# Layer 0 of a two-layer hybrid decoder trunk: VectorE's work, the weight loads and ScalarE's sums in another order up to the scan

## What is computed

```python
h = rmsnorm(x, norm_mix[i])
z = h @ w_in[i]
y_ssm = ssm_branch(z[..., :c0], ...) @ w_ssm_out[i]          # complex diagonal state space model
y_att = dilated_attention(z[..., c0:c1], ..., positions, ...) @ w_att_out[i]   # masks, rotary angles
mem_n = rmsnorm(mem, norm_mem[i])
y_mem = memory_attention(z[..., c3:c4], mem_n, w_mem_kv[i], ...) @ w_mem_out[i]
...
x = x + merged @ w_o[i]
h2 = rmsnorm(x, norm_ffn[i])
x = x + swiglu(...)          # layer 0: dense; layer 1: top 2 of 8 experts
```

## Time and profile before

| | us |
|---|---|
| median of 3 runs | 1813.82 (1813.15 to 1814.66) |
| profiled execution, its own time | 1815.75 |
| its span, first to last instruction | 1813.8 |
| PE busy in the span | 1762.2 (97%) |
| DVE busy | 1442.5 (80%) |
| ACT busy | 1175.7 (65%) |
| mean granted TensorE clock | 0.993 |

### The profile page before, as it was taken

How to read it: one execution, slowest core, us unless ns; L and a number is a source line. 1 busy time by engine, 2 the same in 40 slices (tenths; PEclk the granted TensorE clock), 3 DMA queues, 4 the chain that set the end, 5 groups by cost and what they waited for, 6 DMA issues and landing times.

```text
span 1813.8 us, 23378 instructions
## 1 busy us (share of the span) xinstructions
PE 1762.2 (97%) x8755; PEld 1457.4 (80%) x8755; DVE 1442.5 (80%) x1336; ACT 1175.7 (65%) x1322; POOL 113.9 (6%) x159
## 2 busy tenths in 40 slices
PE   7799999999999999999999999999999999999998
PEld 5687878888887878887888878888878888888886
DVE  7987557677756954668899888898888998988987
ACT  6467564654455665556776767777767767777775
POOL 3341000122001300000000000000000000000000
PEclk9899999999999999999999999999999999999999
DMA  6344434755544443377999999999999999999994
GB/s 207 116 140 139 139 117 161 229 188 185 184 139 142 149 134 132 118 253 290 371 366 335 371 335 365 366 347 354 377 320 372 365 336 372 357 369 373 350 373 186
DMA packets 227630, 477.17 MB, mean 263 GB/s; under 512 B 16012, under 2 KB 40712, under 8 KB 227528
## 3 DMA queue, kind: packets, MB, share of 16 engines
q1 hardware_dynamic: 227144, 474.99, 73.8%
q0 software_dynamic: 288, 0.79, 0.2%
q10 hardware_dynamic: 96, 0.02, 0.0%
HBM read 474.71 MB, written 1.05 MB: 262 GB/s over the span
## 4 chain that ended last, share of the span: by engine, by line
PE 90%; DVE 4%; ACT 2%; issue 1%; SPq 1%; DMA 1%; DVEq 0%; ACTq 0%
PE ps L694 27%; PE ps L696 27%; PE ps L695 27%; PE ps L1175 1%; PE ps L942 1%; DVE lo L2221 1%; PE ps L914 1%; PE ps L1153 1%; PE ps L873 1%; PE ps L687 1%; DVE ring_lo L1823 1%; PE ps L925 1%; DMA ring<-in_w_mem_kv 1%; ACT hi_m L1309 1%; SPq L420 1%
## 5 line engine op out<-in xcount | busy, mean ns | idle before, releaser
L2221 DVE TENSOR_TENSOR lo<-ring_e,hi 128x2048 fp32r<-128x2048 f32 x288 | 657.8, 2290 | 89.9 <-ACT hi L1590 87.7
L1590 ACT ACTIVATE hi<-ring_e 128x2048 fp32r<-128x2048 f32 x288 | 552.0, 1917 | 172.2 <-PE ps L696 171.7
L694 PE MATMUL ps<-hi,xe_hi 128*128 128x512 f32 x896 | 356.4, 398 | 6.9 <-issue 6.9
L696 PE MATMUL ps<-hi,xe_lo 128*128 128x512 f32 x896 | 350.9, 392 | 0.0
L695 PE MATMUL ps<-lo,xe_hi 128*128 128x512 f32 x896 | 350.4, 391 | 0.0
L1309 ACT ACTIVATE hi_m<-ring 128x1024 fp32r<-128x1024 f32 x160 | 160.7, 1054 | 166.0 <-PE ps L696 157.7
L1823 DVE TENSOR_TENSOR ring_lo<-ring,hi_m 128x1024 fp32r<-128x1024 f32 x160 | 190.6, 1233 | 35.0 <-ACT hi_m L1309 34.5
L694 PEld LDWEIGHTS ps<-hi,xe_hi 128*128 128x128 f32 x896 | 169.1, 189 | 43.5 <-issue 8.3
L696 PE MATMUL ps<-hi_m,xT_lo 128*128 128x512 f32 (+1 forms) x528 | 204.0, 386 | 0.0
L696 PEld LDWEIGHTS ps<-hi,xe_lo 128*128 128x128 f32 x896 | 168.9, 189 | 36.6
L695 PEld LDWEIGHTS ps<-lo,xe_hi 128*128 128x128 f32 x896 | 169.2, 189 | 33.5
(11 more groups left out here) (398 smaller groups left out, 2494.4 us busy)
## 6 DMA issues: line engine op xcount, KB each, us to landing
ring_e<-in_moe_w_gate SPq DMA_DIRECT2D x104, 1024.0 KB, 6.7
ring_e<-in_moe_w_up SPq DMA_DIRECT2D x96, 1024.0 KB, 6.8
ring_e<-in_moe_w_down SPq DMA_DIRECT2D x88, 1024.0 KB, 6.2
ring<-in_w_in SPq DMA_DIRECT2D x50, 1024.0 KB, 5.1
hT<-in_moe_w_down SPq DMA_DIRECT2D x24, 1024.0 KB, 6.7
hT<-in_moe_w_up SPq DMA_DIRECT2D x16, 1024.0 KB, 6.0
ring<-in_ffn_w_gate SPq DMA_DIRECT2D x22, 512.0 KB, 4.0
ring<-in_ffn_w_up SPq DMA_DIRECT2D x22, 512.0 KB, 5.0
```

Of the source, the lines that this page charges most:

```text
L694: nc.tensor.matmul(o, x_hi, w_hi, start=first, stop=False, skip_group_check=True)
L696: return nc.tensor.matmul(o, x_lo, w_hi, start=False, stop=end, skip_group_check=True)
L1590: nc.scalar.activation(hi[:, m % H, :], src, ACT.Copy).then_inc(sem("hi_ready"), 1)
L2221: last = V.tensor_tensor(lo[:, m % H, :], src, hi[:, m % H, :].bitcast(F32), ALU.subtract)
```

## The change

It changes the order of work in layer 0 before the scan; no instruction is added or left out. On SP the positions are loaded fourth, before the second half of the small gains, and tile 3 directly after tile 2, ahead of `load_matrices` and of the broadcasts. On VectorE `constants()` and `rotary_angles()` come before `setup()`, and the rest of tile 7 between `table_coarse` and `table_fine`. On ScalarE the sums of squares of the memory tokens stand after the rotary sines, those of `x` after the high part of tile 4; the high part of tile 3 comes ahead of `input_transposed` and `take_memory(0)`. On GpSimd the masks' second bound comes ahead of `ssm_zeros`, and the first part of `second_matrices` ahead of the reciprocal root for `x`.

```diff
@@ block.sync
                 sp.dma_start(par_rows[i * L * KD:(i + 1) * L * KD, :], ...)
+            sp.dma_start(pos_i[:], positions.rearrange("o (c p) -> p (o c)", p=P)).then_inc(sem("pos_loaded"), 16)
...
             sp.dma_start(x[:], x_in[0].rearrange("(c p) d -> p c d", p=P)).then_inc(sem("x_loaded"), 16)
-            load(2, mix_tiles(0)[2])
-            sp.dma_start(pos_i[:], positions.rearrange("o (c p) -> p (o c)", p=P)).then_inc(sem("pos_loaded"), 16)
+            for i in range(2, R + 1):
+                load(i, mix_tiles(0)[i])
             load_matrices(nc.sync, 0)
...
-                    if l > 0 or i >= R:
+                    if l > 0 or i > R:
                         load(BASE[l] + i, src)
@@ block.gpsimd
-            def second_matrices(l):
+            def second_input(l):
...
                 nc.gpsimd.memset(mT[:], 0.0).then_inc(sem("mT_zero"), 1)
+
+            def second_output(l):
+
...
+            pool.wait_ge(sem("grid_ready"), 1)
+            for c in range(C):
+                for g in range(NG):
+                    last = nc.gpsimd.affine_select(out=gmask(c, g), ...)
+            last.then_inc(sem("mask_ready"), 1)
             ssm_zeros(0)
...
             for l in range(L):
+                if l == 0:
+                    second_input(0)
                 rsqrt_mean(rs[:, 2:2 + C], ss[:, 2:2 + C], D, (sem("x_squared"), 2 * l + 1), sem("x_rs"))
                 if l == 0:
-                    pool.wait_ge(sem("grid_ready"), 1)
...
-                    second_matrices(0)
+                    second_output(0)
@@ block.scalar
                     nc.scalar.activation(dt16[:], dt16[:], ACT.Exp).then_inc(sem("dt_ready"), 1)
-                    act.wait_ge(sem("mem_loaded"), 16)
-                    sum_squares(0, h, "mem_squared", z)
-                    act.wait_ge(sem("x_loaded"), 16)
-                    act.wait_ge(sem("mem_squared"), 1)
-                    sum_squares(2, x, "x_squared", z)
                     weights_high(l)
...
                     nc.scalar.activation(rope[:, 0], turns[:], ACT.Sin, scale=-1.0,
                                          bias=half_pi[:]).then_inc(sem("rope_ready"), 1)
+                    sum_squares(0, h, "mem_squared", z)
+                    weights_high(l)
+                    act.wait_ge(sem("mem_squared"), 1)
                     input_transposed()
                     take_memory(0)
-                    weights_high(l)
                     act.wait_ge(sem("transposed_used"), batches_to(l, "h"))
                     from_batch(coefficients_moves)
                     weights_high(l)
+                    sum_squares(2, x, "x_squared", z)
                 weights_high(l)
@@ block.vector
                 state_rates(l)
-                rotary_angles()
                 weights_low(l)
...
                 table_coarse(l)
+                weights_low(l)
                 table_fine()
                 table_folds()

             def ssm(l):
-                weights_low(l)
+                if l > 0:
+                    weights_low(l)
...
+            constants()
+            rotary_angles()
             setup()
-            constants()
             for l in range(L):
                 ssm_setup(l)
```

More of the change, by code:

```diff
@@ L629, in _ @@
                                               base=SPAN - c * P, pattern=[[1, (c + 1) * P]], channel_multiplier=-1))
+            pool.wait_ge(sem("grid_ready"), 1)
+            for c in range(C):
+                for g in range(NG):
+                    last = nc.gpsimd.affine_select(out=gmask(c, g), in_=gmask(c, g), compare_op=ALU.is_ge, fill=NEG,
+                                                   base=c * P, pattern=[[-1, (c + 1) * P]], channel_multiplier=1)
+            last.then_inc(sem("mask_ready"), 1)
             ssm_zeros(0)
@@ L668, in _ @@
                     ssm_zeros(1)
-                    second_matrices(1)
+                    second_input(1)
+                    second_output(1)
                     rotary_gains(1)
@@ L1413, in mixer @@
                     state_steps(l)
-                if l == 0:
                     act.wait_ge(sem("rope_angle_ready"), 1)
```

## The result

The changed kernel is **slower**: 1822.02 us median of 7 runs (1819.62 to 1823.34) against 1814.91 us of the kernel before in the same session (7 runs, 1813.15 to 1816.71). The ratio is 1.0033, with a 95% interval of [1.0023, 1.0042], just above the 0.2% that can be told from no change; in us the interval is 4.2 to 7.6. The forecast was 1813.6 us with a range to 1816.4; both the sign and the size are wrong. The profiled run took 1819.62 us; its span is 1817.7 us, against 1813.8 before.

What follows compares the result with a forecast made beforehand. VectorE's chain before the scan was taken to bound the kernel: its end at 76.3 - 1.1 - 1.0 + 2.3 = 76.5 us, tile 8 ending at 90.4 instead of 90.57, gain 0.2, hence 1813.6 us, range 1809.4 to 1816.4.

Steps and rivals of the forecast that it cites:

- the large wait: TensorE's 9.64 us idle until the rest of tile 7; forecast to move to tile 8 as 10 to 12 us.
- the tail behind F: ScalarE's work after VectorE's last fold; tile 8 can't start before 6.3 us later, then takes 7.6 us.
- F: End of VectorE's nearly gapless work before the scan, at its last fold: 76.3 us before, 76.5 forecast.
- the landing of tile 4: SP's load of tile 4 lands at 37.6 us; ScalarE waits 4.4 us, leaving 1.1 of 5.6 us gained.
- the upper bound of 1.5: Delay of `setup()` on VectorE behind constants and angles: 0.6 us forecast, at most 1.5 if positions land at 7.3.
- The sequence that I copied from the kernel before: SP's six matrix loads, four broadcasts and one tile: 14.5 us from tile 3's landing to tile 4's.
- The second rival: SP held 8.5 us by the second `b` matrix's load; tile 4 lands at 42.3, 1818.3 us; chance 0.1.
- The take-back from GpSimd: Less contention on VectorE as GpSimd's second `b` matrices end before tile 5: 1.0 us gained, bounds 0 and 1.8.
- ScalarE's cover: 1.6 us by which tile 3's first half on ScalarE (25.7) precedes VectorE's need for it (27.3).
- The sums are free: ScalarE's sums of squares of the memory tokens, 4.4 us, moved after the sines, cost no time.

Runs made afterwards that it cites:

- two experiments: Against the changed kernel: tile 3 issued where it was before, 1817.70 us (1.0010 to before); the four broadcasts behind tile 5, 1816.17 us (1.0007).
- The second session: The changed kernel unaltered, timed once more against the kernel before: 1819.45 us median against 1815.52, ratio 1.0027 [1.0016, 1.0038].

## Why the prediction was wrong

**Right in kind.** Constants and angles run in idle time, all but the last 2.0 us; tile 3's high part doesn't wait for DMA and tile 4's does; VectorE's gap is before the rest of tile 4; the large wait moves from tile 7 to tile 8; the tail behind F is as reckoned (tile 8 starts at F + 6.46 against F + 6.3, and lasts 7.37 against 7.6); the rest of tile 7 costs 2.4 of F against 2.3.

**The step that failed is the landing of tile 4**, "tile 4 at 37.6"; it landed at 43.5. Of these 5.9 us:
- *4.1 us: tile 3 lands at 27.2, not 23.1.* The forecast says: "Everything in `setup()`, TensorE's tile 0 and its end at 17.41 moves by this to 18.0." Its end came near 21.8. `setup()` began 2.0 us late, at 10.81, above the upper bound of 1.5: the positions were there (6.72), but the constants took 2.7 us instead of 2.2 and the angles 4.1 instead of 3.0, both now beside GpSimd's masks and fills; the bound was for late positions, and contention wasn't in it. That is 1.4 us more than the forecast's 0.6. Then tile 0's first 11 matmuls ran at half pace, 2.3 us, which the forecast put at nothing; the remaining 0.4 are tile 3's own time (5.4 instead of 5.1) and the reading of 17.41, which is the start of the matmul after tile 0. All of it counts in full, since SP's wait for tile 0 stands ahead of the whole queue.
- *1.8 us: from there to tile 4 it took 16.3 us, not 14.5.* The sequence that I copied from the kernel before was the right one to copy, and still a bound rather than a value: 5.4 us from one landing to the issue of the next tile instead of 4.4, and 10.9 instead of 10.2 from there. The three other traces with this order have 16.2 to 17.2. The second rival's threshold, a landing of 41.4, is passed, but not by its mechanism: the second `b` matrix held SP 3.87 us, not 8.48.

**The take-back from GpSimd was too small.** "I take back 1.0 us ... bounds 0 and 1.8": it was 3.2, since VectorE stood idle for nearly all of GpSimd's second `b` matrices (36.48 to 44.6, 8.1 us where they took 11.1). The forecast's bound came from looking at one slowed instruction; the whole stretch from the rest of tile 4 to the turns was slowed. So F: 76.5 forecast, + 5.9 - 2.2 + 0.1 = 80.3, measured 80.26. This also explains why a tile 4 that came 5 to 7 us earlier in two experiments gained but 1.9 to 3.5: the first 3.2 us are given back as contention.

**ScalarE's cover.** "The sums are free": they are, but they hid tile 0's end. Before, ScalarE is ready for tile 2's high part only at 20.95, so a tile 0 that ends some 3 us later costs nothing; after, it waits 4.84 us for it and VectorE 1.42 behind that.

**The remainder.** The median moved by 7.1 us, the span of the profiled runs by 3.9, the trace at 91 us by 3.5. The second session's difference of medians is 3.9. The ratios' intervals, 4.2 to 7.6 us and 2.9 to 6.9, overlap, so the two sessions may well have measured the same difference. Later shifts in the traces are short stretches at the lower clock that fall elsewhere from one profile to the next: from 1300 to 1350 us the granted clock is 0.97 in the kernel before and 1.00 after. Whether the first session's further 3 us have such a cause isn't settled; the profiled run was the fastest of its seven. Measured against the forecast's 1813.6, the median of 1822.02 is 8.4 us off: 3.7 are the step above with its take-back (94.09 at the end of tile 8 where 90.4 was forecast), 1.1 are that the kernel before itself had a median of 1814.91 over seven runs where the forecast used 1813.82 from three, and 3.6 are this remainder. Besides, the prediction set the span equal to the time of a run, but the profiled run of before took 1815.75, 1.9 more than its span.

## What to carry to other kernels

When a load is moved up in a queue, look at what now stands between it and the *next* one: here the wait only moved from tile 3 to tile 4 and grew, because small broadcasts stayed ahead of the load that became critical. Put slow small loads behind the last load that anything waits for, before moving work between engines: in the changed kernel that alone gave back 2.1 to 3.1 us at R, in the kernel before 1.4, which its timing can't show. And price work that is removed from an engine by what it hid, and an interval by its whole length beside the other engine, not by the one instruction in it that looks slow.

## What the runs showed of the hardware

**Small broadcasts delay a large load behind them.** 128 KB in all (4 of 32 KB), yet a tile behind them lands 5.5 us later (10.9 against 5.4). The six loads of matrices stood ahead of it in both and add little: the tile right behind them takes 5.4 to 7.4 us with no broadcast between, and tile 3, issued to an empty queue in the changed kernel, 5.4. The Trainium skill, "DMA: Bandwidth & Descriptors" (anatomy of one DMA, GpSimd path), gives about 2.0 us plus bytes over 436 GB/s, an estimated 4.4 us for a tile: 1.0 short of 5.4, and far off behind the broadcasts.

**Tile 0 starts at half pace in most profiles.** Its first matmuls after the change, in TensorE's timeline:

```profile
14.30 0.63 PE L702 MATMUL ps<-ring_lo,xT_hi 128*128 128x512 f32 x1
14.73 0.63 PE L703 MATMUL ps<-hi_m,mem_lo 128*128 128x512 f32 x1
15.16 0.63 PE L701 MATMUL ps<-hi_m,xT_hi 128*128 128x512 f32 x1
```

They are 0.43 us apart instead of 0.23, as at tile 8 while 1.2 GHz is granted, although the view by stretch shows a granted clock of 1.00 here; in the changed kernel's second profile it shows 0.57 for 14 to 18 us. Of 14 profiles 12 begin tile 0 so, with 6 to 13 slow matmuls each; tile 0 is 1.3 to 2.7 us longer for it. The two without are the kernel before and the one with the angles after `setup()`, both after a wait of 1.6 to 1.7 us; but four others after 1.5 us have 6 to 8, and the eight after 3.4 to 4.2 us have 7 to 13. So the kernel before's profile, on which I built, was a lucky one. What decides it, no run shows. The Trainium skill, "TensorE: Matmul & The Clock Gate" (what's actually happening), says that the number of slow matmuls at a start varies from run to run of the same kernel, and these profiles agree (11 and 8 in the two of the changed kernel).

**VectorE and GpSimd slow each other, even by a fill.** The angles' `TENSOR_SCALAR` of 128x64 at 9.43 took 1.20 us, in the kernel before 0.20, and it ended at 10.63, when GpSimd's memset did (10.58), in GpSimd's timeline:

```profile
9.63 0.95 POOL L559 MEMSET cT<- 128x1024 f32 x1
...
63.45 2.05 POOL L609 TENSOR_TENSOR cT<-cT,spT 128x1024 f32<-128x1024 f32 x1 [14.34 <-ACT cT L1291]
65.46 1.90 POOL L610 TENSOR_TENSOR gT<-cT,spT 128x1024 f32<-128x1024 f32 x1
```

In five other profiles with the angles in this place it takes 1.46 or 1.47 us and ends with the fill as well. In the kernel before with constants and angles first, GpSimd's two fills lie earlier, at 5.66 to 7.80, and there this operation takes 0.20 again, while two of the constants, in VectorE's timeline, take 1.0 and 1.1 us instead of 0.3:

```profile
5.91 1.00 DVE L1884 TENSOR_SCALAR mask<-grid_i 128x256 f32<-128x256 int32 x1
6.84 1.11 DVE L1883 TENSOR_SCALAR grid_i<-dist_i 128x256 int32<-128x256 int32 x1
```

Beside the last of GpSimd's lines above, and GpSimd's products that follow, the rest of tile 7 took 5.08 us instead of 2.36. The Trainium skill, "SBUF — State Buffer" (two separate sides), says that the two share a port pair which one holds for its whole instruction while the other stands, a VectorE operation with two inputs in SBUF only against a GpSimd one that reads there. The rest of tile 7 has two such inputs and GpSimd's products read there, so that rule fits it; the small operations stretched with the fills as a held port would have it, but have one input, and the fills read nothing, so by the page they would have to be in one of VectorE's two-port modes, which no row shows. Where VectorE stood idle, GpSimd's second `b` matrices were 3.0 us shorter.
